# Norm squares summed on TensorE in four token parts, and the attention woven over two units

## The reference

```
def rmsnorm(x, g):
    y = x * rsqrt(mean(x * x, axis=-1) + EPS);  return y * g
h = modulate(rmsnorm(x, g), shift, scale)            # before each FFN and before the mixing
s = einsum(q, k) * HEAD_DIM ** -0.5                  # two score maps a head, head width 64
p = softmax(s);  p_diff = p[:, :, 0] - lam * p[:, :, 1]
o = rmsnorm(einsum(p_diff, v), g_subln) * (1 - lam_init)
```

## Time and profile before

| | |
|---|---|
| median of 3 runs | 2639.79 us |
| the profiled execution, its span | 2638.57 us, 2636.7 us |
| TensorE busy | 2554.9 us, 97% |
| VectorE busy | 2069.8 us, 79% |
| ScalarE busy | 1012.5 us, 38% |
| GpSimd busy | 163.7 us, 6% |
| mean granted clock of TensorE | 0.994 |

### The profile page before, as it was taken

One profiled execution on the slowest core, in us unless ns is written; L12 is line 12 of the kernel. 1 busy time (PEld: TensorE's weight loads), 2 busy tenths in 40 slices (PEclk: granted clock), 3 DMA queues, 4 the chain that ended last, 5 costly groups with the idle time before them and its releaser, 6 DMA issues. The chain is left out here.

```text
span 2636.7 us, 42699 instructions
## 1 busy us (share of the span) xinstructions
PE 2554.9 (97%) x15356; PEld 2363.0 (90%) x15356; DVE 2069.8 (79%) x3414; ACT 1012.5 (38%) x1854; POOL 163.7 (6%) x314
## 2 busy tenths in 40 slices
PE   6999999999997999999999899999998998999999
PEld 5899999988965889999999799999997866989998
DVE  5688888887958388888888888777768956688885
ACT  4333433333147333422332433234324256344443
POOL 2000000020003200000000200000002003100001
PEclk8999999999999999999999999999999999999999
DMA  8234323332111113333334123343232201223332
GB/s 295 64 120 136 116 92 114 124 104 64 55 57 49 33 56 105 117 93 115 123 103 136 48 90 119 98 130 119 91 104 72 88 24 47 79 83 109 99 101 79
DMA packets 192361, 253.97 MB, mean 96 GB/s; under 512 B 7278, under 2 KB 130268, under 8 KB 192220
## 3 DMA queue, kind: packets, MB, share of 16 engines
q1 hardware_dynamic: 192220, 252.07, 30.4%
HBM read 249.95 MB, written 2.10 MB: 96 GB/s over the span
## 5 line engine op out<-in xcount | busy, mean ns | idle before, releaser
L1211 PE MATMUL ps<-h_hi,w_hi 128*128 128x384 f32 (+2 forms) x2368 | 790.5, 334 | 21.9 <-DVE h_lo L2326 18.2
L1213 PE MATMUL ps<-h_hi,w_lo 128*128 128x384 f32 (+2 forms) x2368 | 785.3, 332 | 0.0
L1212 PE MATMUL ps<-h_lo,w_hi 128*128 128x384 f32 (+2 forms) x2256 | 749.3, 332 | 0.0
L1211 PEld LDWEIGHTS ps<-h_hi,w_hi 128*128 128x128 f32 x2368 | 449.3, 190 | 53.6 <-issue 22.5
L1213 PEld LDWEIGHTS ps<-h_hi,w_lo 128*128 128x128 f32 x2368 | 449.3, 190 | 20.7
L1212 PEld LDWEIGHTS ps<-h_lo,w_hi 128*128 128x128 f32 x2256 | 428.0, 190 | 19.2 <-issue 1.0
L1811 ACT ACTIVATE w_hi<-raw 128x512 fp32r<-128x512 f32 x464 | 279.7, 626 | 420.8 <-PE ps L1213 327.8
L2468 DVE TENSOR_TENSOR w_lo<-raw,w_hi 128x512 fp32r<-128x512 f32 x464 | 307.5, 684 | 14.8 <-ACT w_hi L1811 14.8
L1211 PE MATMUL ps<-t_hi_all,w_hi 128*128 128x384 f32 x864 | 292.1, 338 | 0.0
L1213 PE MATMUL ps<-t_hi_all,w_lo 128*128 128x384 f32 x864 | 292.0, 338 | 0.0
L1212 PE MATMUL ps<-t_lo_all,w_hi 128*128 128x384 f32 x864 | 291.9, 338 | 0.0
(11 more groups left out here) (276 smaller groups left out, 3994.1 us busy)
## 6 DMA issues: line engine op xcount, KB each, us to landing
side_raw<-in_w_ada SPq DMA_DIRECT2D x240, 256.0 KB, 2.7
raw<-in_w_ffn_gate SPq DMA_DIRECT2D x44, 1024.0 KB, 5.4
raw<-in_w_ffn_up SPq DMA_DIRECT2D x44, 1024.0 KB, 5.4
raw<-in_w_ffn_down SPq DMA_DIRECT2D x44, 1024.0 KB, 5.0
raw<-in_w_in SPq DMA_DIRECT2D x14, 1024.0 KB, 5.3
ada_buf<-in_w_ada SPq DMA_DIRECT2D x12, 1024.0 KB, 12.4
raw<-in_w_out SPq DMA_DIRECT2D x8, 1024.0 KB, 5.7
raw<-in_w_in SPq DMA_DIRECT2D x8, 512.0 KB, 7.2
```

Source lines behind the costliest of these rows:

```text
L1211: mm(out, wh, xh, start=start, stop=False, skip_group_check=reopened)
L1212: mm(out, wh, xl, start=False, stop=False, skip_group_check=reopened)
L1213: return mm(out, wl, xh, start=False, stop=stop, skip_group_check=reopened)
```

## The change

For the norms q = 1 to 5 (`between(q)`) GpSimd's additions and `stat` go. TensorE sums the squares itself: for each chunk j four matmuls with 32 columns of ones, each over a quarter of the segment's tokens, into partitions 32c to 32c+31 of one bank, accumulated over the 8 chunks. ScalarE's squares go to four buffers. Root and reciprocal work on n/4 columns. Four further matmuls (`spread`) pick the four parts out with a column of the identity, repeated 128 times, and lay the n reciprocals over all partitions in PSUM, where VectorE's `tn` reads them. The order of the work changes with it:

- after an FFN: chunks 0 to 3 of the first segment are summed behind down chunk 0 of the second segment and 4 to 7 behind chunk 1; `spread` stands behind chunk 3, and behind chunks 3 to 7 one chunk each of the second segment is summed. Its last three stand in the next stage's first pass (k = 0, 1, 2; for q = 2 and 5 the last two at k = 1 and 3), its `spread` at k = 4 (at k = 7 for q = 2 and 5).
- after the mixing: eight chunk sums behind out product 4 of the first segment, one behind 6 and 7, two behind product 4 of the second, `spread` behind its 5, one each behind its 6 and 7.
- VectorE's `split` of the next tile comes after the reciprocal.

In the attention, a latent unit's two maps lie side by side in three banks; even and odd units have a set of three each. The scores are six matmuls of 256 keys; before the fifth TensorE waits until its second is done. One `reduce_max` serves both maps, so both exponentials wait for it. `take_o` goes from VectorE to ScalarE; the squares of four units are one ScalarE instruction, with one sum on VectorE. After `turn_o` ScalarE copies to `a_raw`, which frees bank 6; GpSimd makes `h_hi` from it, VectorE `a_lo`. Of the splits for the out projection only the first stays in the loop; the others follow it. The Fourier stage takes its banks from 3 to 7 instead of 4 to 7.

```diff
+def attention_order(l, i):
+    u, us = i - T_LAG, units_of(l)
+    if i % 2 == 0:
+        want = [("O", u - 1, 0), ("O", u - 1, 1), ("T", u, 0)]
+    else:
+        want = [("T", u - 1, 1), ("O", u - 1, 0), ("T", u, 0), ("O", u - 1, 1), ("T", u, 1)]
...
+            def sum_squares(q, s, js):
+                o, n = PIECES[s][:2]
+                bank = bank_of(("stat", q, s))
+                for j in js:
+                    if j == 0:
+                        wait_bank(pe, ("stat", q, s))
+                    pe.wait_ge(sq_done, sqcount(q, s, j))
+                    for c in range(4):
+                        at_ = n // 4 * c
+                        last = mm(ps[32 * c:32 * c + 32, bank, 0:n // 4], ones[:, 0:32], square_of(q, s, j)[:, at_:at_ + n // 4],
+                                  start=(j == 0), stop=(j == KD - 1), skip_group_check=True)
+                    if j < 4:
+                        last.then_inc(sq_summed, 1)
+                    elif j == KD - 1:
+                        last.then_inc(products, 1)
+            def spread(q, s):
+                n = PIECES[s][1] // 4
+                wait_bank(pe, ("spread", q, s))
+                pe.wait_ge(rstd_ready, rstd_number(q, s))
+                for c in range(4):
+                    last = mm(ps[:, bank_of(("spread", q, s)), n * c:n * c + n], ident[:, 32 * c:32 * c + 1].to_broadcast([128, 128]),
+                              fourths(q, s, rstd4), start=True, stop=True, skip_group_check=True)
+                last.then_inc(products, 1)
...
+                        if s == second and after < 3 * DEPTH:
+                            a_, b_ = seg_order(after)
+                            if j < 2:
+                                sum_squares(after, a_, range(4 * j, 4 * j + 4))
+                            if j == 3:
+                                spread(after, a_)
+                            if j >= 3:
+                                sum_squares(after, b_, (j - 3,))
...
-                    parts = [(st, 2 * mine[st] + half, 384 * half, 384) for half in range(2) for st in range(2)]
+                    parts = [(0, 0, 0, 0, 256), (1, 1, 256, 0, 256), (0, 0, 256, 256, 256), (1, 2, 0, 256, 256),
+                             (0, 1, 0, 512, 256), (1, 2, 256, 512, 256)]
...
                 for i in attention_steps(l):
+                    if i < len(us):
+                        score(l, i)
                     if pair_turned(l, i) is not None:
                         turn_o(l, pair_turned(l, i))
+                    for what, u, half in attention_order(l, i):
+                        if what == "T":
+                            turn_p(u, half)
+                        else:
+                            heads(u, half)
```

ScalarE's list in the attention:

```diff
+                    if i % 2 == 0:
+                        take_o(i - O_LAG - 1)
+                        late_p(i - T_LAG - 1, 1)
+                        if EARLY_UNITS <= i - 1 < len(us):
+                            exponent(i - 1, 1)
+                        if pair_turned(l, i) is not None:
+                            head_raw(pair_turned(l, i))
+                        if i < len(us):
+                            exponent(i, 0)
+                        take_o(i - O_LAG)
+                        if 0 <= i - O_LAG < len(us) and (i - O_LAG) % BATCH == BATCH - 1:
+                            square_heads(i - O_LAG)
+                        late_p(i - T_LAG, 0)
+                        if i < len(us):
+                            exponent(i, 1)
+                    else:
+                        late_p(i - T_LAG - 1, 1)
+                        late_p(i - T_LAG, 0)
+                        if i < len(us):
+                            exponent(i, 0)
```

VectorE's:

```diff
+                for i in range(EARLY_UNITS, len(us) + OT_LAG + 1):
                     if i < len(us):
                         maximum(i)
                     if 1 <= i <= len(us):
                         combine(i - 1)
+                    if 0 <= i - O_LAG < len(us) and (i - O_LAG) % BATCH == BATCH - 1:
+                        sum_heads(i - O_LAG)
+                    if pair_turned(l, i - 1) is not None:
+                        head_low(pair_turned(l, i - 1))
+                    if i == 5:
+                        split(("out", l, 0))
+                split(("out", l, 1))
+                split(("out", l, 2))
```

More of the change, by code:

```diff
@@ L230, in __init__ @@
         self.build()
+        self.compact()
         self.occupants()
@@ L239, in slot, with next_bank, open, close @@
         self.uses[bank] += 1
+        if bank in self.held:
+            self.spread_before[key] = self.held.pop(bank)
+    def next_bank(self):
+        while self.bank in self.blocked:
+            self.bank = (self.bank + 1) % 8
+        bank = self.bank
+        self.bank = (bank + 1) % 8
+        return bank
+    def open(self, q, s):
+        bank = self.next_bank()
+        self.slots[("stat", q, s)] = (None, bank, self.uses[bank])
+        self.uses[bank] += 1
+        self.blocked.add(bank)
+        if bank in self.held:
+            self.spread_before[("stat", q, s)] = self.held.pop(bank)
+    def close(self, q, s):
+        _, bank, use = self.slots[("stat", q, s)]
+        self.slots[("stat", q, s)] = (self.n, bank, use)
+        self.n += 1
+        self.blocked.remove(bank)
+    def spread(self, q, s):
+        self.slot(("spread", q, s))
+        bank = self.slots[("spread", q, s)][1]
+        self.uses[bank] -= 1
+        self.blocked.add(bank)
+    def unblock(self, q, s):
+        bank = self.slots[("spread", q, s)][1]
+        self.blocked.remove(bank)
+        self.held[bank] = (q, s)
     def tile(self, key, split=True):
@@ L334, in side, with first_sums, renumber @@
             self.slot(("side", f, n), (self.bank + ahead) % 8)
-    def second_stat(self, f, key):
-        w = STAT_AT[f] and STAT_AT[f][0][0]
-        if f and key == (w, f, 0, 0, last_slots(f)[0]):
-            q = (0, 2, 3, 5)[f]
-            self.slot(("stat", q, seg_order(q)[1]))
+    def first_sums(self, f, w, k):
+        q = (0, 2, 3, 5)[f]
+        second = seg_order(q)[1]
+        if 7 in sums_first(w, k, f):
+            self.close(q, second)
+        if (w, k) == (SUM_PASS[f], SPREAD_AT[f]):
+            self.spread(q, second)
+    def renumber(self, keys):
+        for key in keys:
+            _, bank, use = self.slots[key]
+            self.slots[key] = (self.n, bank, use)
+            self.n += 1
     def ffn(self, f):
@@ L406, in mix @@
             self.tile(("K", l, v))
-        for s in (1, 0):
-            for h in range(HEADS):
-                self.slot(("K", l, h, s))
+        q = 3 * l + 1
+        keys = [("K", l, h, 1) for h in range(HEADS)]
+        for key in keys:
+            self.slot(key)
+        self.close(q, 0)
+        self.spread(q, 0)
+        self.renumber(keys)
+        self.unblock(q, 1)
+        for h in range(HEADS):
+            self.slot(("K", l, h, 0))
+            if h % 2:
+                pass
+        self.unblock(q, 0)
         for v in range(2):
@@ L847, in addcount @@
             o = square_order(q)
+            assert not between(q)
             last = ADDED if q == 3 * DEPTH else KD
-            return 14 * q + sum(1 for x in o[:o.index((s, j)) + 1] if 0 < x[1] < last)
+            return (14 if q else 0) + sum(1 for x in o[:o.index((s, j)) + 1] if 0 < x[1] < last)
         def square_of(q, s, j):
             o, n = PIECES[s][:2]
+            if between(q):
+                return sq4[:, j % 4, o:o + n]
             if j == 0:
@@ new lines, in heads @@
+                def heads(u, half):
+                    h, s, t = us[u]
+                    wait_freed(pe, ("T", l, u, half))
+                    if half == 0:
+                        wait_bank(pe, ("O", l, u))
+                    for k in range(3 * half, 3 * half + 3) if s == 0 else range(4, 6):
+                        last = mm(ps[:, 7, 0:128], pT[:, u % 2, k if s == 0 else k - 4, :],
+                                  vN[:, k, 128 * h:128 * h + 128], start=(k == (0 if s == 0 else 4)), stop=(k == 5), skip_group_check=True)
+                    if half == heads_end(l, u):
+                        last.then_inc(products, 1)
@@ L2030, in ffn @@
                     square(q, first, j)
-                if nxt:
-                    split(nxt[1])
-                for j in range(2):
-                    square(q, second, j)
                 if not nxt:
-                    for j in range(2, KD - 2):
+                    for j in range(KD - 2):
                         square(q, second, j)
@@ L2041, in ffn @@
                     return
+                square(q, second, 0)
                 root(q, first)
+                split(nxt[1])
+                square(q, second, 1)
                 square(q, second, 2)
@@ L2750, in ffn @@
                         add_one(j, second)
-                    split(nxt[1])
-                    add_one(2, second)
                     last_seg = second
```

331 lines of the change are left out of this document (201 added, 130 removed).

## The result

The changed kernel takes 2667.49 us (median of 5 runs, 2667.17 to 2668.47); the kernel before, run beside it, 2638.39. The ratio is 1.0111 with a 95% interval of 1.0097 to 1.0126: the change makes the kernel 1.1% slower. The forecast was 2637.5 us in a range of 2622 to 2650, so it missed by 30 us and the time lies outside the range. The profiled execution has a span of 2666.7 us, 30.0 more than before. TensorE is busy for 2583.7 us (2554.9 before). So 28.8 us of the difference are more work, which includes products at half clock, and 1.2 us are more idle time.

The account below looks back on a forecast made before the run. TensorE was taken as the bound, by its work, idle time and time at the lower clock. The profiled 2638.57 us, +11.3 for the norms and -12.0 for the attention, gave 2637.9, called 2637.5, range 2622 to 2650.

Parts of the forecast that it names:

- all of these waits: Norms: TensorE's standstills in q = 1, 3, 4, remaining `sqsum` waits and lost clock all go, 25.4 us in sum.
- The norms: Norms q = 1 to 5: 36.7 us of added TensorE work less 25.4 us removed, a net loss of 11.3 us.
- the attention: Both layers' attention: new order, moved splits and loop tail, less new waits, a net gain of 12.0 us.
- a lone group: Norms: one chunk's squares summed alone between other products costs 0.56 us with 128 columns, 0.40 with 64.
- A spread: Norms: the 8 records laying the reciprocals over all partitions cost 1.0 us with entry.
- The runs: Norms: groups of squares standing together cost 0.28 us each plus 0.2 for the run.
- (b): In the down product and out product 4, each group of squares pays entry even in a run: 2649 us; chance 0.17.
- (d): In the norms, groups of squares are as cheap alone as in a run, 0.23 us: 2623 us; chance 0.10.
- The splits with the tail: Attention: two splits moved out of each loop, with the loops' tail, gain 4.4 us; the `w_lo` wait costs 0.7.
- the weave with its wait for bank 3: Attention: the new order gains 7.3 us in layer 0, 2.1 in layer 1; first scores' wait for bank 3 costs 1.1.
- (a): In the attention, the weave removes nearly all waits, gaining 25 us instead of 12: 2625 us; chance 0.18.
- (c): The attention gains nothing, since maximum and `combine` in series set the pace: 2650 us; chance 0.13.

Follow-up runs that it names:

- e1: The changed kernel with two PSUM banks chosen otherwise (latent keys of head 1; second segment's up product in q = 3); 2639.9 us, ratio 1.0010.
- e3: The kernel before with the change's norms alone, using e1's banks so that no bank collision is in it; 2642.3 us, ratio 1.0012.
- e2: The kernel before with the change's attention alone, its norms as they were; 2630.4 us, ratio 0.9976.
- e9: e7 with the weight splits of out products 1 and 2 back inside the attention's loop; 2627.1 us, ratio 0.9961.
- e7: e1 with twenty VectorE memsets and their spare buffer added, TensorE summing squares only in norms q = 1, 3 and 4; 2621.2 us, ratio 0.9940.
- e14: e1 with twenty VectorE memsets added and the shared region 128 bytes higher than in the kernel before; 2621.2 us, ratio 0.9936.
- e13: The kernel before with an unused buffer that puts the shared region 128 bytes higher, nothing else; 2627.8 us, ratio 0.9961.
- e5: e1 with one VectorE memset more, of a spare column, behind the first feed-forward's loop; 2636.5 us, ratio 1.0001.

## Why the prediction was wrong

**The failed step.** "Laid out for q = 1 in this trace's time, the first `h_lo` is ready at about 581.4 us ... the second segment's first is ready at 597.6 for a need at 601.0. So I take all of these waits as gone". The operands were ready as laid out, even earlier (594.8 instead of 597.6 for the second segment). The layout asked only for operands. A product also needs its PSUM bank, and the part of the change that opens and blocks banks shifts every bank behind it. The two lists that would have told were at hand: the order of banks in the plan, and ScalarE's order, with `high` and a split ahead of the key copies. In the kernel before ScalarE begins those copies at 610.78 us, 10 us after TensorE begins the latent keys, which no one notices as long as the banks differ. Cost: 22.2 us of stalls and 6.4 of clock by the timelines, 27.6 by e1. Without it the time would have been 2639.9, and the forecast 2637.5. That these two lie so close is luck: three misses cancel. The norms were put 6.7 us too dear (11.3 for 4.6), the attention 4.7 us too good (12.0 for 7.3), and 4.5 us of stalls by VectorE stood in no term at all.

**The norms' other terms.** The price of a lone group held: it moves the next product by 0.55 us (0.56 forecast) with 128 columns and by 0.43 (0.40) with 64. A spread moves it by 0.9 (1.0). The runs were priced too high: a run of four adds 0.8 us (1.3 forecast), a run of eight 1.6 in q = 2 and 1.2 in q = 5 (2.4 forecast). Two groups of 128 columns that stand together cost 0.8 and not 1.1. So q = 1 adds about 6.1 us net of the two `stat` where 7.7 stood. By the forecast's own terms q = 1, 3 and 4 had to come out at -0.7, +0.9 and +0.1 us; e3 shows -2.7, -2.4 and -2.5. The 1.6 us of work account for about half of the gap or more; what is left, 0.4 to 1.7 us a norm, was being lost there beyond the waits and the clock read from the earlier trace rows, and was not traced. For q = 2 and 5 together 6.9 + 6.6 - 2.5 = 11.0 us of loss stood, and 8.5 were measured. How much the norms lose as a whole stays loose: +4.6 by e3's median, +0.8 by their places in its trace, +11.3 in the forecast. Rivals (b) and (d), which differ in the price of a group, both fall: a lone group costs 0.55 and one in a run 0.2.

**The attention.** 7.3 us by e2 for 12.0, and about 5.5 without the clock. The splits with the tail, net of the wait on `w_lo`, were put at 3.7. They measure 5.9 in the new order (e9 against e7) and about 4 without the clock, so this term was about right. What fell short is the weave with its wait for bank 3: 7.3 + 2.1 - 1.1 = 8.3 stood, and 5.5 - 4 leaves 1 to 2 us, an estimate from these runs, unless the splits cost the old loop less than the new one, which no run separates. A head takes 21.9 us for the 21.2 laid out, and its waits end as forecast in `pT` (11.8 us over both layers). In layer 1 nothing is left: the loop is 1.2 us shorter, or some 3 without the place at the lower clock in it, and a wait of 1.56 us ahead of it (1.1 forecast) and one of 1.4 on `w_lo` (0.7 forecast) take that back. Rivals (a) and (c) bracket it, neither right.

**The two terms that stood in no list.** VectorE's loop across a block (4.5 us of TensorE's time by its timeline in e1's placement; the medians of e1, e14 and the two kernels before allow up to 9), and the address. At equal placement and without the collision the whole change is worth 2627.8 - 2621.2 = 6.6 us of gain (e13, e14), with a mean granted clock of 0.992 and 0.996. That is less than the 10.8 us that one unused buffer makes.

## What to carry to other kernels

When a change takes a bank, a buffer or a slot out of a ring, write out who follows whom in each place of the ring, and when the engine that empties it comes to it in its own list. "The operand is ready" is half of a start. A wait put down to `issue` right behind products of another segment can be a resource freed late, and so can a wait put down to an operand that was long ready: look for the drain that ends just before it. Before comparing two versions by less than half a per cent, give both the same start of the buffers TensorE reads and the same place of hardware loops in each engine's program, or the placement decides; and compare the granted clock stretch by stretch, since one place at the lower level was worth 1.7 us here.

## What the runs showed of the hardware

- A start of the shared region 128 bytes higher makes the same products follow one another 0.9% faster (0.1750 to 0.1734 us) and the kernel before 10.8 us quicker (2638.6 to 2627.8); 32 bytes higher makes the step longer (0.1755).
- A VectorE loop of 320 instructions costs 5.5 us at a turn when it starts at instruction 1465 and 0.4 when it starts at 1466 (e1, e5); a loop of 290 costs 2.9 to 3.2 us or 0.4 to 0.5, again by its start.
- A standstill of 7 us of TensorE in these norms was followed by products of 512 columns at 0.63 us instead of 0.39, a granted clock at its lower level; waits of 1.99 us did the same before. Not every such wait did: in the kernel before, those of 2.31 us at 1469.54 and 2.07 us at 2002.09 were followed by products at full pace.
- The granted clock also fell in places that a run left untouched, and not in every execution: the same scores took 2.51 us in e3 and 1.56 in the kernel before. Each place cost about 1.7 us.
